# A hybrid decoder layer on one core: first convolution sums in PSUM, first rows among keys and values, feed-forward pairs among the rows, last rows weighted ahead

## What is computed

```python
mem_n = rms_norm(mem, mem_norm)
h = rms_norm(x, mix_pre_norm)
z = h @ w_in                          # pooling, conformer, short gated convolution
ya = pool_mixer(zp, pool_maps, pool_scale)
yb = conformer_conv(za, zg, ...)      # a * sigmoid(gate), causal conv of 31 taps, layer norm, silu
yc = zb * causal_dwconv(zc * zx, sconv_w)
x = x + rms_norm(concat(ya, yb, yc) @ w_out, mix_post_norm)
h = rms_norm(x, xattn_pre_norm)
x = x + rms_norm(cross_attention(h, mem_n, wq, wk, wv, wo), xattn_post_norm)
h = rms_norm(x, ffn_pre_norm)
u = causal_dwconv(h @ w_up, w_conv)   # 3 taps over 2 x 2816 channels
x = x + rms_norm((silu(gate) * val) @ w_down, ffn_post_norm)
```

## Time and profile before

| | |
|---|---|
| median of 3 runs | 2662.65 us (2659.29 to 2666.55) |
| profiled execution | 2663.32 us, span 2661.0 us |
| granted clock of TensorE, mean | 0.986 |
| TensorE busy | 2545.3 us (96%) |
| VectorE busy | 1519.8 us (57%) |
| ACT busy | 917.7 us (34%) |
| GpSimd busy | 857.7 us (32%) |

### The profile page before, as it was taken

How to read it: one execution, slowest core, us unless ns; L and a number is a source line. 1 busy time by engine, 2 the same in 40 slices (tenths; PEclk the granted TensorE clock), 3 DMA queues, 4 the chain that set the end, 5 groups by cost and what they waited for, 6 DMA issues and landing times.

```text
span 2661.0 us, 32853 instructions
## 1 busy us (share of the span) xinstructions
PE 2545.3 (96%) x11713; PEld 2113.1 (79%) x11713; DVE 1519.8 (57%) x2446; ACT 917.7 (34%) x1515; POOL 857.7 (32%) x346
## 2 busy tenths in 40 slices
PE   7869899999999999999999999999999999999997
PEld 6657788878877888887888878888878888778886
DVE  3898888777837434436526366256365264562462
ACT  5323222232234333333423333334334333333332
POOL 5451410000013000014534444544445444345342
PEclk9979999999999999999999999999999999999999
DMA  7795585674858766746333253332353332433331
GB/s 234 230 329 188 187 313 183 223 290 178 311 189 341 260 253 244 265 146 198 106 92 95 86 186 102 111 88 95 97 182 111 87 96 88 151 111 111 88 95 64
DMA packets 313813, 452.59 MB, mean 170 GB/s; under 512 B 12072, under 2 KB 234557, under 8 KB 292669
## 3 DMA queue, kind: packets, MB, share of 16 engines
q1 hardware_dynamic: 305101, 438.56, 48.8%
q10 hardware_dynamic: 8560, 12.06, 1.4%
HBM read 368.78 MB, written 81.79 MB: 169 GB/s over the span
## 4 chain that ended last, share of the span: by engine, by line
PE 84%; DVE 9%; issue 3%; ACT 1%; DMA 1%; POOL 1%; DVEq 0%; ACTq 0%; SPq 0%; POOLq 0%
PE colb L1442 17%; PE colb L1444 17%; PE colb L1443 17%; PE accb L1442 11%; PE accb L1444 11%; PE accb L1443 11%; DVE arena L1174 3%; PE colb L1479 2%; DVE arena L1114 1%; PE accb L1642 1%; POOL pair L627 1%; DMA raw<-in_xattn_wq 1%; DVE small L1035 1%; ACT junk L679 1%; ACT pair L658 0%
## 5 line engine op out<-in xcount | busy, mean ns | idle before, releaser
L627 POOL TENSOR_TENSOR pair<-raw,pair 128x1024 fp32r<-128x1024 f32 x339 | 856.7, 2543 | 1772.7 <-ACT pair L658 1772.4
L1442 PE MATMUL colb<-hT,pair 128*128 128x512 f32 x1952 | 766.0, 392 | 18.8 <-issue 15.4
L1443 PE MATMUL colb<-hT,pair 128*128 128x512 f32 x1952 | 762.6, 391 | 0.0
L1444 PE MATMUL colb<-hT,pair 128*128 128x512 f32 x1952 | 762.5, 391 | 0.0
L658 ACT ACTIVATE pair<-raw 128x1024 fp32r<-128x1024 f32 x339 | 355.4, 1052 | 479.7 <-PE accb L1444 276.9
L1385 DVE TENSOR_SCALAR arena<-arena,par 128x512 f32<-128x512 f32 x176 | 245.9, 1437 | 376.2 <-ACT arena L965 375.7
L1442 PE MATMUL accb<-pair,act 128*128 128x512 f32 x1120 | 440.6, 393 | 16.7 <-POOL pair L627 5.9
L1442 PEld LDWEIGHTS colb<-hT,pair 128*128 128x128 f32 x1952 | 368.5, 189 | 103.6 <-issue 27.8
L1444 PE MATMUL accb<-pair,act 128*128 128x512 f32 x1120 | 437.7, 391 | 0.0
L1443 PE MATMUL accb<-pair,act 128*128 128x512 f32 x1120 | 437.6, 391 | 0.0
L1444 PEld LDWEIGHTS colb<-hT,pair 128*128 128x128 f32 x1952 | 368.1, 189 | 77.2
(11 more groups left out here) (152 smaller groups left out, 2325.6 us busy)
## 6 DMA issues: line engine op xcount, KB each, us to landing
pair<-kept SPq DMA_DIRECT2D x123, 1024.0 KB, 5.0
raw<-in_ffn_w_up SPq DMA_DIRECT2D x176, 512.0 KB, 3.8
raw<-in_ffn_w_down SPq DMA_DIRECT2D x176, 256.0 KB, 2.9
kept<-pair SPq DMA_DIRECT2D x41, 1024.0 KB, 6.1
raw<-in_w_in SPq DMA_DIRECT2D x17, 512.0 KB, 7.2
xh<-in_x SPq DMA_DIRECT2D x4, 2048.0 KB, 14.1
xt<-in_x SPq DMA_DIRECT2D x4, 2048.0 KB, 15.3
x_mixed<-xt SPq DMA_DIRECT2D x4, 2048.0 KB, 11.5
```

Source lines behind the costliest of these rows:

```text
L627: nc.gpsimd.tensor_tensor(pair[:, b, 1, :], raw[:, r, :], pair[:, b, 0, :].bitcast(F32), ALU.subtract).then_inc(lo_done, 1)
L1442: nc.tensor.matmul(dst, sh, mh, start=first, stop=False)
L1443: nc.tensor.matmul(dst, sh, ml, start=False, stop=False)
L1444: return nc.tensor.matmul(dst, sl, mh, start=False, stop=last)
```

## The change

Four edits.

1. In PREP the two alternating sums of the convolution lie in PSUM banks 2 and 3 of `accb` (`SUM_BANKS`); the last multiply-add of a chunk writes `cacc`, and the closing addition reads the other sum from PSUM. The A rows of MIX_FIRST use banks 0 and 1 twice (`a_bank`), and the later uses of `accb` in that stage count one more (`later_use`).
2. In PREP GpSimd waits until the memory rows are scaled. ACT takes the first rows' squares after keys 0 to 3, and places two weight roundings before and amid the memory rows. VectorE makes the root during keys 4 to 7 and scales a block of rows after each of values 0 to 3. TensorE transposes the maps after value 3, waits for the rows, and transposes two of the eight row groups after each of values 4 to 7.
3. The feed-forward pairs are a function (`ffn_pair`). `new_rows` of the last attention tile and of feed-forward tiles 0 to 2 calls it for pairs 0 to 3 of the next tile: pair 0 after the first block is weighted, then block 1 weighted and block 0 added, pair 1, and so on. SP's feed-forward program is written out for four tiles; the store of the tile before and the load of the gain stand at slot 8, the load of the old rows at slot 10, the load of the next rows stays at slot 0.
4. In the last tile the result of the first half of the columns (all blocks), and of the second half for blocks 0 and 1, is multiplied by the gain into `xh` before the root (`gain_rows`). After the root, blocks 0 and 1 take one operation each, blocks 2 and 3 three operations of 512 columns (`last_rows`).

```diff
+    SUM_BANKS = (2, 3)
@@ gpsimd
+            pool.wait_ge(h_ready, 1)
             for p in (PREP, MIX_FIRST):
@@ scalar, keys of PREP
             for i in range(KD):
                 key_values(0, i)
-            sc.wait_ge(xh_in, 16)
-            for r in range(RB):
-                square(xh[:, r, :], ssx[:, r:r + 1], PREP, 0, M // P + r)
+                if i == 0:
+                    sc.wait_ge(xh_in, 16)
+                if i < RB:
+                    square(xh[:, i, :], ssx[:, i:i + 1], PREP, 0, M // P + i)
@@ vector, keys and values of PREP
             for i in range(KD):
-                key_values(0, i, KD + i)
+                key_values(0, i)
+                if i == KD // 2:
+                    ve.wait_ge(act_step, M // P + RB)
+                    rsqrt_begin(ssx[:, 0:RB], D)
+                elif i > KD // 2:
+                    rsqrt_round(rh[:, 0:RB], i - KD // 2 - 1)
             for i in range(KD):
-                key_values(1, i, 2 * KD + i)
-                if i == 3:
-                    ve.wait_ge(act_step, M // P + RB)
-                    scale_rows(RB)
+                key_values(1, i)
+                if i < RB - 1:
+                    first_row(i)
+                elif i == RB - 1:
+                    first_row(i).then_inc(h_ready, 1)
@@ vector, new_rows
                 for r in range(RB):
+                    if between is not None and r:
+                        between(r - 1)
                     step(nc.vector.scalar_tensor_tensor(y[:, r, :], y[:, r, :], rs[:, r:r + 1], gain[:, :], ALU.mult, ALU.mult))
                     if r:
                         settle(1)
-                        added = nc.vector.tensor_tensor(xt[:, r - 1, :], xt[:, r - 1, :], y[:, r - 1, :], ALU.add)
-                        if by_row:
-                            added.then_inc(x_new, 1)
+                        nc.vector.tensor_tensor(xt[:, r - 1, :], xt[:, r - 1, :], y[:, r - 1, :], ALU.add)
+                if between is not None:
+                    between(RB - 1)
                 settle()
@@ vector, conformer
-                    sums = [cacc[:, j, :], ct[:, 0, 0:T]]
+                    sums = [accb[b][:, :] for b in SUM_BANKS] if p == PREP else [cacc[:, j, :], ct[:, 0, 0:T]]
@@
-                            step(nc.vector.scalar_tensor_tensor(sums[k % 2], src, w, sums[k % 2], ALU.mult, ALU.add))
+                            total = cacc[:, j, :] if k == TAPS - 1 else sums[k % 2]
+                            step(nc.vector.scalar_tensor_tensor(total, src, w, sums[k % 2], ALU.mult, ALU.add))
                     settle()
-                    step(nc.vector.tensor_tensor(cacc[:, j, :], cacc[:, j, :], ct[:, 0, 0:T], ALU.add))
+                    step(nc.vector.tensor_tensor(cacc[:, j, :], cacc[:, j, :], sums[1], ALU.add))
@@ vector, last tile
+            def last_rows(t):
+
+                root_of_result(FFN, t)
+                ve.wait_ge(xt_in, step_tile.at(FFN, t, 1) * 16)
+                for r in range(RB):
+                    cols = slice(0, D if r < YG1 else T)
+                    ins = nc.vector.scalar_tensor_tensor(xt[:, r, cols], xh[:, r, cols], rs[:, r:r + 1], xt[:, r, cols], ALU.mult, ALU.add)
+                    if r >= YG1:
+                        step(ins)
+                        rest_ = y_ffn[:, r, T:D]
+                        chain(nc.vector.scalar_tensor_tensor(rest_, rest_, rs[:, r:r + 1], gain[:, T:D], ALU.mult, ALU.mult))
+                        ins = nc.vector.tensor_tensor(xt[:, r, T:D], xt[:, r, T:D], rest_, ALU.add)
+                    ins.then_inc(x_new, 1)
@@ tensor, values of PREP
+            for i in range(KD):
+                column_slot(PREP, 0, place[PREP]["v", i], item[PREP]["v", i], memT, M)
+                if i == KD // 2 - 1:
+                    pe.wait_ge(maps_in, 16 * NW)
+                    transposes(PREP, 0, item[PREP]["bd",], [bd[:, e, :] for e in range(NP_)]).then_inc(xp_full, 1)
+                    pe.wait_ge(h_ready, 2)
+                if i >= KD // 2:
+                    for k in range(2 * (i - KD // 2), 2 * (i - KD // 2) + 2):
+                        head(PREP, 0, item[PREP]["row", k], k)
```

More of the change, by code:

```diff
@@ L114, in build @@
                 [("r", i) for i in range(2, RSLOTS)] + [("row", k) for k in range(KD)] + [("crow", j) for j in range(NC_)]
-    PREP_ITEMS = [("par",)] + [("mem", k) for k in range(KD)] + [(what, i) for what in "kv" for i in range(KD)] + [("bd",)] +\
-                 [("row", k) for k in range(KD)] + [("c", i) for i in range(CSLOTS)] +\
+    PREP_HIS = [("mem", k) for k in range(KD)] + [("k", i) for i in range(KD)] + [("v", i) for i in range(KD // 2)] + [("bd",)] +\
+               sum([[("v", KD // 2 + i), ("row", 2 * i), ("row", 2 * i + 1)] for i in range(KD // 2)], [])
+    PREP_ITEMS = [("par",)] + PREP_HIS + [("c", i) for i in range(CSLOTS)] +\
                  [("pooled", half, c) for half in range(2) for c in range(NP_)]
@@ L609, in _ @@
                 body(ATTN, t)
-            with sp.Fori(0, NT - 1) as t:
+            for t in range(NT):
                 body(FFN, t)
-            body(FFN, NT - 1)
             sp.wait_ge(x_stored, 16 * (1 + 3 * NT - 1 + RB))
@@ L1025, in rsqrt, with rsqrt_begin @@
             def rsqrt(dst, total, count):
+                rsqrt_begin(total, count)
+                for k in range(3):
+                    rsqrt_round(dst, k)
+            def rsqrt_begin(total, count):
                 n = total.shape[-1]
@@ L1110, in new_rows @@
                 rsqrt(rs, rs, D)
+            def new_rows(p, t, y, between=None):
+                root_of_result(p, t)
                 ve.wait_ge(gain_in, step_tile.at(p, t, 1) * 16)
@@ L1556, in a_rows @@
                     copied(("T", g, 1))
-                    acc_is_free(p, t, A_USE, g)
+                    bank, use = a_bank(p, g)
+                    acc_is_free(p, t, use, bank)
                     for k in range(2):
@@ L1560, in a_rows @@
                             o = (HC * k + m) * P
-                            ins = products(accb[g][:, k * M:(k + 1) * M], [act[:, e, WQT + g % 2, o:o + P] for e in range(2)],
+                            ins = products(accb[bank][:, k * M:(k + 1) * M], [act[:, e, WQT + g % 2, o:o + P] for e in range(2)],
                                            [act[:, e, HEAD_KV, m * M:(m + 1) * M] for e in range(2)], m == 0, m == HC - 1)
@@ L1604, in out @@
                     units = [(Y_ORDER[2 * j + e], j + e == 0, 2 * j + e == KD - 1, act) for e in range(2)]
-                    row_slot(p, t, place[p]["out", half, j], units, (OUT_USE + half, None))
+                    row_slot(p, t, place[p]["out", half, j], units, (later_use(p, OUT_USE) + half, None))
                 for j in range(2):
```

233 lines of the change are left out of this document (139 added, 94 removed).

## The result

| | before | after |
|---|---|---|
| median | 2663.37 us (4 runs on this chip) | 2623.92 us (4 runs, 2623.67 to 2625.01) |
| profiled execution: span | 2661.0 us | 2622.0 us |
| granted clock of TensorE, mean | 0.986 | 0.989 |
| VectorE / GpSimd busy | 1519.8 / 857.7 us | 1514.3 / 846.1 us |

The ratio is 0.9856, with a 95% interval of 0.984 to 0.9872. The changed kernel is faster by 39 us.

The account below looks back on a forecast made before the run. TensorE was taken as the bound (84% of the last chain), so only its waits and low clock could be won. Span 2661.0 - 36 (parts 1, 2) - 0 (part 3) - 2.5 (part 4) = 2622.5; forecast 2625 us, range 2606 to 2643.

Parts of the forecast that it names:

- the front: From the start to the transposes of the first convolution's sums: these start at 158.5 instead of 193.91, 35.4 us earlier.
- Sums in PSUM: First convolution: taps take 0.66 us from start to start even beside splits; VectorE ends at c+81 to c+82.
- TensorE from c to the sums' transposes: First convolution: TensorE's own work from the first column slot takes 83.5 us, so it arrives about 2 after VectorE.
- Rows among keys and values: PREP before the convolution: the new order starts the first column slot at 74.7 instead of 86.53, 11.8 us earlier.
- of the kind of the 2.24: A new TensorE wait for the first rows after the fourth value, charged 2 us like the existing one at 86.53.
- the low bound of 8: Least gain in us at the first column slot, if each row scaling is shut out for a split and TensorE waits.
- Pairs between rows: Four feed-forward boundaries: first rounding 7.8 us earlier, but pairs 1 to 3 take 13.5 each; gain 0 (+5 to -15).
- rival (a): Feed-forward boundaries: the gaps are real and each gives back 6 us or so; 2601 to 2611 us, chance 0.15.
- Last rows: End of the last tile: row operations after the root take 6.6 to 7 us instead of 9.4; gain 2.5.
- (c): First convolution: VectorE reading and writing one PSUM bank is costly; slower, 2680 us at 1.5 us a tap; chance 0.03.
- (d): First convolution: the sums aren't the cause, TensorE is late for another reason; 2650 to 2660 us, chance 0.04.
- Rival (b): Front gives less: TensorE meets the DMA or taps cost 0.79 to 0.9; sums end 165 to 172; 2632 to 2640; chance 0.18.

Follow-up runs that it names:

- e1: The changed kernel with the first convolution's two sums in SBUF again, all else as changed; 2648.22 us, ratio to before 0.9956.
- e5: The changed kernel with TensorE's wait for the scaled first rows moved behind the fifth value's products; 2621.84 us, ratio to before 0.9846.
- e10: The same kernel as e5, measured once more in five rounds; 2621.92 us, ratio to before 0.9861.
- e7: The changed kernel with the edits of e5 and e6 together; 2628.54 us, ratio to before 0.9872.
- e0: The changed kernel as it is, measured again as the mark for the follow-up runs; 2624.68 us, ratio to before 0.9868.
- e8: The changed kernel with GpSimd splits of half the size in the feed-forward stage, low parts left out, for time alone; 2609.34 us, ratio to before 0.9813.
- e6: The changed kernel with row addition and halo copy written as operations of two tensors and a scalar; 2626.12 us, ratio to before 0.9853.

## Why the prediction was right, step by step

The time was 2623.92 us, 2625 had been said, and the span fell by 39.0, where the sum had 38.5. But the terms didn't all come out: the front gave 8.1 us less than the sum had (27.3 for 35.4), by two errors, and it is luck that as much came back elsewhere. The mechanisms of parts 1, 3 and 4 held; sizes in the front were off.

- **Sums in PSUM.** 0.66 us from start to start beside splits, splits of 2.4: as predicted, and e1 shows it as the cause. With c as in the prediction (the start of the first column slot, 79.62 in the kernel after) the sums ended at c + 81.7 (161.36), as said; TensorE, not VectorE, came last. The estimate by the Trainium skill (VectorE: DVE Perf Modes, TRN2 errata: 62 cycles more for a source in PSUM, 4.4 us here) does not agree with the trace, 747 ns for a tap with PSUM, 746 for the operation from PSUM to SBUF and 741 without PSUM.
- **TensorE from c to the sums' transposes.** 83.5 said (79 to 88); 87.0 measured, and 84.8 to 89.1 in the eleven traces that have the sums in PSUM. From 86.5 up the wait for the keys' transfer is 3.2 to 4.4 us, below that 1.3 to 1.5. I had charged the DMA 1.5 further on; its share in 120 to 160 us was 0.98 after against 0.74. This term was 1.3 to 5.6 too small, 3.5 in the profile of the result.
- **Rows among keys and values.** The memory rows came at 11.98, 12.2 said. The failed step is the new wait, "of the kind of the 2.24": taken as 2, it was 5.12. With 2.0 for the lower clock behind it (60.5 to 64.6) that is about the missing 4.9 of c, 79.62 for 74.7; c came 6.9 us earlier than before, less than the low bound of 8. The low bound had named the cause (each scaling shut out for a split), and the sum left it out, though the rows showed it for the memory rows. Where part of it is hidden behind products, in e5, e10 and e7, c is 73.62, 72.39 and 75.35, and the transposes come at 158.5, 159.0 and 161.9; 74.7 and 158.5 had been said. So the front gave 27.3 (26.4 to 29.6 in seven traces) instead of 35.4.
- **What made it good.** Up to the first attention tile the lead grows to 31.2 (32.4 in e0): 2.1 is the lower clock behind the old wait, which the sum had; the rest (1.8 and 0.7) differs from one execution to the next, as the wait of 1.9 or 4.2 us in that tile does, and no part of the change aimed at it. Then come 1.5 because no lower clock follows that wait in this execution, which e0 doesn't show, and 3.3 in the feed-forward stage, 0 said, within its bounds.
- **Pairs between rows.** The first rounding of a tile came 8.2 to 8.6 us earlier, 7.8 said. Pairs of 13.4 us, 13.5 said; the next 11.98, 12.2 said; the eleventh rounding 133.3 to 134.0 us behind the root's first operation, 0.6 to 1.1 less than before. So the gaps did mislead, as the text had it: rival (a) did not come, and e8 shows why and what it needed. By the Trainium skill (SBUF — State Buffer, section "SBUF: two separate sides") a VectorE instruction with two SBUF inputs and a GpSimd instruction that reads SBUF exclude each other, and the first to start goes first; e6 agrees (the addition is held in either form, 3.43 us), and the sum rested on that.
- **Last rows.** 2.5 said, 3.0 measured; 6.6 us of row operations, "6.6 to 7" said.
- **Rivals (c) and (d)** are out by the taps and by e1. Rival (b), a front that gives less, is what happened in part. Of its reasons TensorE's meeting the DMA shows (4.4 us for the keys' transfer, 2.4 before); a tap didn't cost 0.79, and the sums ended at 161.36, not at 165 to 172.

## What to carry to other kernels

Where VectorE and GpSimd both work from SBUF, ask of each VectorE instruction with all its tensors in SBUF whether a split is running when it starts, however small it is: here the price was the rest of the split. Moving the accumulators of a long chain to free PSUM banks took the chain out of that contest and was worth 23.5 us (e1). A wait of the bottleneck engine belongs behind all of its work that doesn't need what it waits for; and a gap of the bottleneck engine is only worth what the loop behind it lets it keep.

## What the runs showed of the hardware

- A VectorE chain with one source and the output in the same PSUM bank runs at 0.66 us a step of 512 columns, beside GpSimd splits of 2.4 us; with both sources in SBUF it runs at 0.81, and a split takes up to 8.8 us in the first convolution (e1, at 175.7) and 15.3 in the second tile's (before, at 302.32).
- A copy of 4 columns, 0.17 us alone, took 2.36 beside a split, and so did the small operations on 4 columns in the root (2.40 at 816.18 in the kernel after).
- The form with two tensors and a scalar is held like the addition of two tensors: 3.43 us for both.
- Halving the splits of a stage in which GpSimd was busy 637 of 1419 us took 23.7 us off that stage (15.8 off the span, the rest lost ahead of it), though by the shares of the page GpSimd is far from being a bound.
